# Two FFN down projections of 512 x 2816 x 1024 as seven quadrant products each, one level of Strassen

## The chip, the cores and the metric

The program runs on one core of a Trainium2 chip. The metric is the device time of one execution in microseconds (us). The engines that the text names are TensorE (PE, with its weight loads as PEld), VectorE (DVE), ScalarE (ACT), GpSimd (POOL) and SyncE (SP, which here only issues DMAs).

## The reference

The network is one hybrid block followed by a two-layer block. The change touches only the feed-forward part of the second block:

```python
def conv_ffn(h, w_up, conv_w, conv_b, w_down):
    up = h @ w_up
    a, bval = up[..., :D_FF], up[..., D_FF:]
    a = causal depthwise conv of a, width 3, + conv_b
    return (jax.nn.silu(a) * bval) @ w_down          # D_FF = 2816, D_MODEL = 1024

for l in range(2):                                   # 512 tokens
    ... x = x + mixed @ w_out[l]
    h = rms_norm(x, norm_ffn[l])
    x = x + conv_ffn(h, w_up[l], conv_w[l], conv_b[l], w_down[l])
return rms_norm(x, norm_final)
```

All of it is float32. The product `(silu(a) * bval) @ w_down` has 512 tokens, 2816 = 22 x 128 inner columns and 1024 outputs, and there are two of them, one for each layer.

## The kernel before

**Float32 by three passes.** Every operand of a large matrix product is split into two parts, hi (a rounded copy) and lo (the original minus hi). Both parts are held as `float32r`. `passes` (L1810 to L1814) then issues three matmuls: hi by hi, hi by lo and lo by hi. So one 128 x 128 by 128 x 512 product costs three matmuls of 512 columns.

**Weights.** `weight_plan` cuts all weights into chunks. Each chunk is one DMA, mostly 1 MB, and it holds one or two pieces of 128 x 1024 words. SP loads the chunks in the plan's order into two buffers of `raw` (`chunk_load`, L605 to L609). A load waits until the last piece of the chunk two before it has its lo part. ACT makes the hi part of each piece (`split_hi`, L490 to L497), and DVE makes the lo part from `raw` and hi (`split_lo`, L499 to L505). Both go into one of four slots of `whl`. `room_for` lets ACT write piece w once PE has used piece w - 4. Every loop on ACT and DVE calls the split of piece w + 3 when it stands at piece w, so the splits run up to three pieces ahead of PE.

**Up tiles.** For each f2 of 11, PE makes four tiles: `up_a` of columns 2 f2 and 2 f2 + 1, then `up_b` of the same. Each tile is 24 matmuls. ACT copies `up_a` to `apad`, DVE runs the three conv steps (L1782 to L1784), and ACT applies SiLU into `fsil`. DVE multiplies by `up_b` (L1791), ACT writes the hi part into `ff` (L1062) and DVE the lo part (L1793). `ff` is 88 KB of the 96 KB arena in each partition.

**Down projection.** `row_tiles` (L1841) computes 512 x 1024 outputs in eight PSUM banks, one for each of four token blocks (tb) and two column halves. The token block is the stationary operand, and 512 columns of weights are the moving one. One piece holds two inner tiles of one column half, so PE spends 2 x 4 x 3 = 24 matmuls on each piece. In the second half the last eight inner tiles are done token block by token block, so that each row block ends at a different time. `add_rows` (L1549) adds each bank to the residual `x` on DVE. The norm that follows works row block by row block, and PE transposes the rows (L1836) between the row blocks. In the last layer ACT sums squares (L1068 and L1073), POOL takes the root (L668), and ACT and DVE scale the two halves and store them.

**Queues.** POOL has almost nothing in its queue: the roots of the norms (L668, 28 of them), one early split (L672) and one DMA for each layer (L677). SP's queue holds the weight loads in order, and every load stands behind the wait of the one before it.

Of the kernel before, what the change touches and what calls it, by code (L numbers as in the profile page):

```python
# [31 lines left out]
P = 128  # L32
D = 1024
# [9 lines left out]
FT = D_FF // P  # L43
HEAD = 64
# [55 lines left out]
def weight_plan():  # L100
# [34 lines left out]
    for l in range(LAYERS):  # L135
# [17 lines left out]
        rows("w_down_2", l, FT)  # L153
# [3 lines left out]
def build(nc, t, out):  # L157
# [16 lines left out]
    NP_ = len(pieces)  # L174

# [80 lines left out]
    assert at[0] <= top, at[0] - top  # L256
    sel_r = nc.alloc_sbuf_tensor_at("sel_r", [P, 2, P], R, offset=cst_at + 4 * COFF["sel"])
# [76 lines left out]
    ff = over("ff", 0, [P, FT, 2, SEQ], R)  # L334
    xn2 = over("xn2", 88 * K, [P, 2, D])
# [25 lines left out]
    with ctx:  # L361
# [9 lines left out]
        raw_in, s_raw0 = [sem("raw_in0"), sem("raw_in1")], sem("raw_in_first")  # L371
# [73 lines left out]

        def raw_view(w):
# [3 lines left out]
            r = raw[:, c % 2, :]  # L450
# [5 lines left out]
            if kind in ("w_out", "w_out_2", "w_down_2", "dvw"):  # L456
                return r[:, j * 1024:(j + 1) * 1024].rearrange("p (a b) -> p a b", a=2)
# [32 lines left out]
        def split_hi(w):  # L490

            if w >= NP_:
                return
            c = pieces[w][0]
            nc.scalar.wait_ge(raw_in[c % 2], 16 * (c // 2 + 1))
            room_for(w)
            nc.scalar.activation(whl_view(w, 0), raw_view(w), ACT.Copy).then_inc(w_hi, 1)  # L497
# [11 lines left out]

        def resident(stage):  # L510

            name, l, nk = stage
            return W[(name, l, 1, nk - 8)]
# [21 lines left out]
        def row_wait(eng, stage, half, tb):  # L535
# [4 lines left out]
            elif tb < 3:  # L540
                eng.wait_ge(row_full, ROWS.index(stage) * 6 + half * 3 + tb + 1)
# [39 lines left out]
        def chunk_src(c):  # L581
# [10 lines left out]
            if kind in ("w_out", "w_out_2", "w_down_2"):  # L592
# [68 lines left out]
        def _(pool):  # L661
# [3 lines left out]

            for i_, (s, tb) in enumerate(ORDER):
# [7 lines left out]
                if s in (2, 4) and tb == 3:  # L674
                    l = s // 2 - 1
                    pool.wait_ge(v_out, 32 * (l + 1))
                    pool.dma_start(vc[:].rearrange("p r g n -> p (r g n)"), v_dram[l].rearrange("(u r) n -> u (r n)", r=TB)).then_inc(v_class, 16)  # L677


        @block.scalar  # L680
        def _(act):
# [184 lines left out]
            def norm(s):  # L866
# [35 lines left out]
                norm_hi(s, 3)  # L902

            for l in range(LAYERS):
# [136 lines left out]
                for f2 in range(FT // 2):  # L1041
# [15 lines left out]
                    for j in range(2):  # L1057
                        f = 2 * f2 + j
                        key = ("up_b", l, f)
                        split_hi(W[key] + 3)  # L1060
                        await_read(act, key)
                        A(ff[:, f, 0, :], fsil[:, j, :], ACT.Copy).then_inc(ff_hi, 1)  # L1062
                lead(lead_keys(("w_down_2", l, FT)))
            for tb in range(TB):
                act.wait_ge(row_read, row_reads(ROWS[-1], 0, tb))
                if tb >= 2:
                    act.wait_ge(s_sq0, tb - 1)
                A(xn2[:, 0, tb % 2 * 512:tb % 2 * 512 + 512], x[:, tb, 0:512], ACT.Square, accum_out=ssq0[:, tb:tb + 1]).then_inc(s_sq0, 1)  # L1068
            ov = out[0].rearrange("(b p) d -> p b d", p=P)
            act.wait_ge(s_sq0, TB)  # L1070
            for tb in range(TB):
                act.wait_ge(x_ready, 4 * (STAGES - 3) + tb + 1)
                A(xn2[:, 0, tb % 2 * 512:tb % 2 * 512 + 512], x[:, tb, 512:], ACT.Square, accum_out=ssq[:, tb:tb + 1]).then_inc(s_ssq, 1)  # L1073
# [1299 lines left out]
```

## Time and profile before

| | us |
|---|---|
| median of 3 runs (2155.8 to 2156.01) | 2156.01 |
| the profiled execution | 2156.16 |
| its span | 2154.3 |

| engine | busy us | share of the span |
|---|---|---|
| PE | 2129.8 | 99% |
| DVE | 1276.6 | 59% |
| ACT | 781.4 | 36% |
| POOL | 26.6 | 1% |

The busy time of PE is that of overlapping matmuls. How many microseconds of PE a matmul is worth is read from the distance between two starts, not from its duration. The granted TensorE clock is at its full level (9 in tenths, which is 90% or more) in all 40 slices of the page. DMA moves 101 GB/s on average. In the waits, "A <- B" means that A was idle until B released it.

### The profile page before, as it was taken

The page shows a single profiled execution, that of the slowest core. Times are in us where ns is not written, and L with a number is a line of the kernel's source. Part 1 is how long each engine was busy: PE and PEld are TensorE (multiplying, and loading weights), DVE is VectorE, ACT ScalarE, POOL GpSimd, SP SyncE. Part 2 cuts the span into 40 slices and gives each one's busy share as a digit, 9 for nine tenths or more (in the row PEclk, how much of TensorE's full clock was granted, in tenths as well). Part 3 has the DMA queues.
Part 4 walks back from the last instruction along what each step waited for, and adds up shares of the span by engine and source line. Part 5 has one row for each costly group of instructions (what it writes and reads, how often), then busy time and mean ns, then how long its engine had stood idle before and what let it go on. Part 6 is the DMA issues. An engine that isn't in the chain of part 4 may idle for free.

```text
span 2154.3 us, 24865 instructions
## 1 busy us (share of the span) xinstructions
PE 2129.8 (99%) x10315; PEld 1757.6 (82%) x10315; DVE 1276.6 (59%) x1649; ACT 781.4 (36%) x1036; POOL 26.6 (1%) x41
## 2 busy tenths in 40 slices
PE   7999999999999999999999999999999999999998
PEld 4888888888888887888888888888788888888887
DVE  6899897953665848535665554234853566555422
ACT  3323232223343344444343333135444434333312
POOL 1000000000000100000000000000000000000000
PEclk9999999999999999999999999999999999999999
DMA  9432232233332322322223233223231222323222
GB/s 315 146 118 84 98 103 83 98 117 98 98 93 95 111 79 79 130 67 94 83 84 113 79 109 103 91 69 98 79 137 61 97 78 91 105 83 113 99 88 78
DMA packets 181588, 217.73 MB, mean 101 GB/s; under 512 B 3932, under 2 KB 153316, under 8 KB 181220
## 3 DMA queue, kind: packets, MB, share of 16 engines
q1 hardware_dynamic: 178080, 209.47, 29.5%
q10 hardware_dynamic: 2948, 4.52, 0.6%
q8 instruction: 82, 1.34, 0.3%
q0 software_dynamic: 448, 2.15, 0.3%
q14 instruction: 30, 0.25, 0.0%
HBM read 211.93 MB, written 4.19 MB: 100 GB/s over the span
## 4 chain that ended last, share of the span: by engine, by line
PE 94%; DVE 4%; issue 1%; DMA 1%; ACT 1%; POOL 0%; SPq 0%; POOLq 0%; ACTq 0%; DVEq 0%
PE psum L1812 30%; PE psum L1813 30%; PE psum L1814 30%; DVE whl L504 1%; PE psum L2225 1%; DMA ada<-in_w_ada 1%; PE psum L2257 1%; PE psum L2237 1%; PE psum L2180 0%; PE psum L2210 0%; PE psum L2196 0%; PE psum L1836 0%; PE psum L1955 0%; DVE mrow L1686 0%; POOL stat L668 0%
## 5 line engine op out<-in xcount | busy, mean ns | idle before, releaser
L1812 PE MATMUL psum<-hT,whl 128*128 128x512 f32 (+1 forms) x2064 | 789.1, 382 | 2.8 <-DVE whl L504 1.5
L1814 PE MATMUL psum<-hT,whl 128*128 128x512 f32 (+1 forms) x2064 | 783.1, 379 | 0.0
L1813 PE MATMUL psum<-hT,whl 128*128 128x512 f32 (+1 forms) x2064 | 783.0, 379 | 0.0
L504 DVE TENSOR_TENSOR whl<-raw,whl 128x1024 fp32r<-128x1024 f32 x361 | 438.5, 1217 | 419.5 <-ACT whl L497 419.3
L497 ACT ACTIVATE whl<-raw 128x1024 fp32r<-128x1024 f32 x361 | 376.8, 1047 | 421.3 <-PE psum L1814 386.8
L1812 PEld LDWEIGHTS psum<-hT,whl 128*128 128x128 f32 x2064 | 388.1, 188 | 83.4 <-issue 6.7
L1814 PEld LDWEIGHTS psum<-hT,whl 128*128 128x128 f32 x2064 | 388.2, 188 | 73.7
L1813 PEld LDWEIGHTS psum<-hT,whl 128*128 128x128 f32 x2064 | 388.3, 188 | 71.2 <-issue 0.2
L1812 PE MATMUL psum<-whl,ff 128*128 128x512 f32 x352 | 137.1, 389 | 0.0
L1814 PE MATMUL psum<-whl,ff 128*128 128x512 f32 x352 | 136.9, 389 | 0.0
L1813 PE MATMUL psum<-whl,ff 128*128 128x512 f32 x352 | 136.9, 389 | 0.0
L1812 PE MATMUL psum<-whl,hT 128*128 128x512 f32 (+1 forms) x320 | 112.2, 351 | 0.2 <-DVE whl L504 0.2
L1813 PE MATMUL psum<-whl,hT 128*128 128x512 f32 (+1 forms) x320 | 111.0, 347 | 0.0
L1814 PE MATMUL psum<-whl,hT 128*128 128x512 f32 (+1 forms) x320 | 111.0, 347 | 0.0
L1251 DVE SCALAR_TENSOR_TENSOR hc<-glu,vcol,hc 128x512 f32<-128x512 f32 x120 | 89.9, 750 | 0.0
L1782 DVE TENSOR_SCALAR facc<-apad,vcol 128x512 f32<-128x512 f32 x44 | 24.0, 546 | 110.9 <-ACT fsil L1056 53.0
L1251 DVE SCALAR_TENSOR_TENSOR acc<-glu,vcol,acc 128x512 f32<-128x512 f32 x112 | 84.0, 750 | 0.1
L1050 ACT ACTIVATE apad<-psum 128x512 f32<-128x512 f32 x44 | 26.4, 599 | 146.0 <-PE psum L1814 146.0
L1814 PEld LDWEIGHTS psum<-whl,ff 128*128 128x128 f32 x352 | 66.1, 188 | 13.8
L1813 PEld LDWEIGHTS psum<-whl,ff 128*128 128x128 f32 x352 | 66.1, 188 | 13.7
L1812 PEld LDWEIGHTS psum<-whl,ff 128*128 128x128 f32 x352 | 66.1, 188 | 13.5
L1812 PEld LDWEIGHTS psum<-whl,hT 128*128 128x128 f32 x320 | 60.6, 189 | 8.5 <-issue 0.8
(309 smaller groups left out, 2106.9 us busy)
## 6 DMA issues: line engine op xcount, KB each, us to landing
raw<-in_w_in SPq DMA_DIRECT2D x87, 1024.0 KB, 5.1
raw<-in_w_up SPq DMA_DIRECT2D x44, 1024.0 KB, 5.1
raw<-in_w_down SPq DMA_DIRECT2D x20, 1024.0 KB, 5.0
raw<-in_w_branch SPq DMA_DIRECT2D x12, 1024.0 KB, 5.1
raw<-in_w_out SPq DMA_DIRECT2D x12, 1024.0 KB, 5.0
ada<-in_w_ada SPq DMA_DIRECT2D x8, 1024.0 KB, 9.7
ada<-in_w_ada SPq DMA_DIRECT2D x8, 512.0 KB, 11.1
x<-in_x SPq DMA_DIRECT2D x4, 512.0 KB, 5.6
```

The costliest lines, as they stand in the source:

```text
L497: nc.scalar.activation(whl_view(w, 0), raw_view(w), ACT.Copy).then_inc(w_hi, 1)
L504: nc.vector.tensor_tensor(whl_view(w, 1), raw_view(w), whl_view(w, 0).bitcast(F), ALU.subtract).then_inc(w_lo, 1)
L1050: A(apad[:, j, 2:], bank(W_BANK[key]), ACT.Copy).then_inc(act_read, 1)
L1251: last[dst is acc1] = step(V.scalar_tensor_tensor(A_(dst), g[:, k:k + SEQ], col("cf_w", 8 * k + tt), A_(dst), ALU.mult, ALU.add))
L1782: link(V.tensor_scalar(facc[:], apad[:, j, 2:2 + SEQ], cw(2), col("conv_b", FT * l + f), ALU.mult, ALU.add))
L1812: M(out_, stat_hi, mov_hi, start=start, stop=False, **kw)
L1813: M(out_, stat_hi, mov_lo, start=False, stop=False, **kw)
L1814: return M(out_, stat_lo, mov_hi, start=False, stop=stop, **kw)
L2225: ins = M(bank(2 + e)[:, a:z], qd[heads, g, j, b * P:(b + 1) * P], kd[heads, g, j, k0:k0 + z - a], start=True, stop=True, skip_group_check ...
L2237: ins = nc.tensor.transpose(bank(tb + e)[:, c * P:(c + 1) * P], prob[:, e, c * P:(c + 1) * P], ident)
L2257: ins = M(o_, v, probT[:, e, c * P:(c + 1) * P], start=c in (first_, 2), stop=c in (1, 3), skip_group_check=True)
```

## The change

**Seven products.** The inner tiles are taken in 11 pairs kk, an even tile (t = 0) and an odd one (t = 1). Tokens are cut in halves of 256, output columns in halves of 512. B(t, h) is the 128 x 512 quadrant of the weights in tile t and half h. For each pair there are four kinds of pieces:

- `sA`: B(0, 0) and B(1, 0), as loaded. Two products, with tokens 0 to 255.
- `sB`: T1 = B(0, 1) - B(0, 0), and T4 = B(1, 1) - B(1, 0) - T1. Two products, with tokens 256 to 511, where the even tile's half has been replaced by the sum of the even and odd tiles.
- `sC`: T2 = B(0, 0) + T3, and B(1, 1). Two products, with token sums.
- `sD`: T3 = B(1, 1) - B(0, 1). One product, with a token sum. A piece of `sD` holds two pairs, one of them only one.

A product is two token blocks by three passes, so 6 matmuls of 512 columns. PE's order in `quad_tiles` is all `sA` and `sB` in turn, then all `sC`, then all `sD`.

**Who makes the weight sums.** POOL makes T1 and T4 with two instructions of 1024 and 512 columns, the second behind the first. DVE makes T3 with one of 512 columns, behind the lo part of `sA`. POOL makes T2 in place with one of 512 columns, after all T1 and T4. The splits of all pieces stay on ACT and DVE.

**Loads.** A `quad` chunk (1 MB) holds all four quadrants of a pair and serves `sA`, `sB` and T3. It goes to one of three raw buffers, the third of which lies in the space of `hT` and is free only after the last up tile. Its buffer is released when T1, T4 and T3 are made. `diag` chunks (1 MB for two pairs, by two DMAs) load B(0, 0) and B(1, 1) again for `sC`.

**Token sums.** In the up tiles DVE makes, for each f2, four more instructions (256, 256, 512 and 768 columns) and ACT one of 768. POOL stores the 768 KB that result to DRAM. ACT loads them back into the place of `ff` tiles that PE is done with, one for each pair, during `sA` and `sB`.

**Residual.** `x` (2 MB) goes to DRAM at the start of the up tiles, its space serves for sums, and POOL loads it back after its third T1 and T4. Partial sums of PSUM are added to `x` between the products.

```diff
+        for kk in range(PAIRS):
+            add("w_down_2", ("quad", l, kk), [("sA", l, kk), ("sB", l, kk)], 1024)
+        for i in range(0, PAIRS, 2):
+            add("w_down_2", ("diag", l, i), [("sC", l, k) for k in range(i, min(i + 2, PAIRS))], 1024)
...
     def split_hi(w):
+            if key[0] == "sB":
+                nc.scalar.wait_ge(t_sum, PAIRS * key[1] + key[2] + 1)
+            elif key[0] == "sC":
+                nc.scalar.wait_ge(t2_done, PAIRS * key[1] + key[2] + 1)
+            elif key[0] == "sD":
+                nc.scalar.wait_ge(t3_done, PAIRS * (key[1] + 1))
...
+            def raw_released(c):                                   # SP, before a load
+                if held[0] == "quad":
+                    sp.wait_ge(t_sum, PAIRS * held[1] + held[2] + 1)
+                    sp.wait_ge(t3_done, PAIRS * held[1] + held[2] + 1)
+                elif held[0] == "diag":
+                    sp.wait_ge(w_lo, W[("sC", held[1], min(held[2] + 1, PAIRS - 1))] + 1)
...
+                def t1_and_t4(kk):                                 # GpSimd
+                    pool.wait_ge(raw_in[RAW_BUF[c]], RAW_NEED[c])
+                    if kk == 0: ...                                # x stored and its norm done
+                    elif kk == 1:
+                        pool.wait_ge(w_used, W[("up_b", l, FT - 1)] + 1)
+                    elif kk > 2:
+                        pool.wait_ge(w_lo, W[("sB", l, kk - 2)] + 1)
+                    nc.gpsimd.tensor_tensor(tsum_of(kk), q[:, :, 1, :], q[:, :, 0, :], ALU.subtract).then_inc(pool_chain, 1)
+                    pool.wait_ge(pool_chain, PAIRS * l + kk + 2)
+                    nc.gpsimd.tensor_tensor(tsum_of(kk)[:, 1, :], tsum_of(kk)[:, 1, :], tsum_of(kk)[:, 0, :], ALU.subtract).then_inc(t_sum, 1)
+                def t2(kk):
+                    pool.wait_ge(t3_done, PAIRS * l + kk + 1)
+                    nc.gpsimd.tensor_tensor(b11, b11, t3_of(kk), ALU.add).then_inc(t2_done, 1)
+                for kk in range(PAIRS - 1):
+                    store(kk)
+                t1_and_t4(0)
+                t1_and_t4(1)
+                store(PAIRS - 1)
+                t1_and_t4(2)
+                pool.wait_ge(s_stored, 16 * PAIRS * (l + 1))
+                pool.wait_ge(w_lo, W[("sB", l, 0)] + 1)
+                pool.dma_start(x[:]..., x_dram[l]).then_inc(x_moved, 16)
+                for kk in range(3, PAIRS):
+                    t1_and_t4(kk)
+                for kk in range(PAIRS):
+                    t2(kk)
...
+                for w in range(W[("sA", l, 0)], W[("sC", l, PAIRS - 1)] + 1):     # VectorE, quad_rows
+                    split_lo(w + 3)
+                    if ahead == ("sB", l, 1):
+                        t3(0)
+                        t3(1)
+                    elif ahead[0] == "sA":
+                        t3(ahead[2])
+                    ...                                            # adds of PSUM banks to x
...
+                    V.tensor_tensor(fsil[:, 0, 256:], fsil[:, 0, 256:], fsil[:, 1, 256:], ALU.add).then_inc(s_sums, 1)
+                    link(V.tensor_tensor(ssum[:, 0:256], fsil[:, 0, 256:], fsil[:, 0, 0:256], ALU.subtract))
+                    V.tensor_tensor(ssum[:, 256:768]..., ALU.subtract).then_inc(s_sums, 1)
+                    V.tensor_tensor(sstage[:, 1, :], ssum[:], sstage[:, 0, :].bitcast(F), ALU.subtract).then_inc(s_lo, 1)
...
+                def sums_back(kk):                                 # ScalarE
+                    act.wait_ge(w_used, W[("sB", l, kk)] + 1)
+                    act.wait_ge(s_stored, 16 * (PAIRS * l + kk + 1))
+                    if kk >= 2:
+                        act.wait_ge(s_back[kk % 2], back_count(l, kk - 2))
+                    act.dma_start(ff_r[:, kk, 0:1536].bitcast(F), s_dram[l, kk]).then_inc(s_back[kk % 2], 16)
...
+                def whole_row(tb):                                 # VectorE, rows 2 and 3, after sD
+                    add(tb, 0, 6 + i).then_inc(quad_read, 1)
+                    add(tb, 1, 6 + i).then_inc(x_ready, 1)
...
-                row_tiles(("w_down_2", l, FT), lambda k: ff[:, k, 0, :], lambda k: ff[:, k, 1, :], (ff_lo, FT * l))
+                quad_tiles(l)
```

## Rows read from the trace of the kernel before

**Rows 1.** The page: PE in the down projections, the first of three passes.

```profile
L1812 PE MATMUL psum<-whl,ff 128*128 128x512 f32 x352 | 137.1, 389 | 0.0
```

**Rows 2.** Windows: both up stages and both down stages, busy time of each engine.

```profile
core 0: us, PE busy (x) PEld busy (x) DVE busy (x) ACT busy (x) POOL busy (x), PEclk, DMA share, GB/s
1093.00:1328.80 235.80, 235.53 (x1111) 197.94 (x1110) 129.16 (x156) 82.74 (x111) 0.00 (x0) 1.00 0.30 99
1328.80:1449.00 120.20, 120.20 (x540) 99.71 (x539) 33.10 (x34) 29.27 (x31) 1.65 (x3) 1.00 0.26 88
2027.00:2147.60 120.60, 120.60 (x533) 99.85 (x532) 34.63 (x40) 27.48 (x37) 1.65 (x3) 1.00 0.26 90
```

**Rows 3.** Timeline of PE in layer 0's down projection: start, us, engine, line.

```profile
1446.20 0.39 PE L1814 MATMUL psum<-whl,ff 128*128 128x512 f32 x1
...
1449.83 0.39 PE L1812 MATMUL psum<-whl,ff 128*128 128x512 f32 x1
```

**Rows 4.** Groups by line and shape, DVE and POOL: count, busy us, mean ns, idle before.

```profile
L504 DVE TENSOR_TENSOR whl<-raw,whl 128x1024 fp32r<-128x1024 f32 x357 | 435.8, 1223 | 419.5 <-ACT whl L497 419.3
L1793 DVE TENSOR_TENSOR ff<-fsil,ff 128x512 fp32r<-128x512 f32 x44 | 30.5, 693 | 30.8 <-ACT ff L1062 30.8
L1558 DVE SCALAR_TENSOR_TENSOR x<-psum,x 128x512 f32<-128x512 f32 x32 | 21.3, 686 | 24.0 <-PE psum L1814 24.0
L672 POOL TENSOR_TENSOR whl<-raw,whl 128x512 fp32r<-128x512 f32 x1 | 1.3, 1275 | 13.3 <-DVE stat L1164 13.3
```

**Rows 5.** Timeline of POOL: four of its 28 roots, and its one wide instruction.

```profile
25.81 1.27 POOL L672 TENSOR_TENSOR whl<-raw,whl 128x512 fp32r<-128x512 f32 x1 [13.28 <-DVE stat L1164]
719.07 1.52 POOL L668 TENSOR_TENSOR stat<-stat 128x1 f32<-128x1 f32 x1 [691.98 <-DVE stat L1109]
737.01 1.46 POOL L668 TENSOR_TENSOR stat<-stat 128x1 f32<-128x1 f32 x1 [5.55 <-DVE stat L1472]
751.38 0.55 POOL L668 TENSOR_TENSOR stat<-stat 128x1 f32<-128x1 f32 x1 [8.13 <-DVE stat L1472]
1440.19 0.55 POOL L668 TENSOR_TENSOR stat<-stat 128x1 f32<-128x1 f32 x1 [4.90 <-DVE stat L1472]
```

**Rows 6.** Timeline of DVE at the same five moments.

```profile
26.78 0.85 DVE L1188 TENSOR_TENSOR hT<-utmp,hT 128x512 fp32r<-128x512 f32 x1
...
718.90 1.28 DVE L1508 SCALAR_TENSOR_TENSOR x<-x,stat,lnrow 128x1024 f32<-128x1024 f32 x1
...
736.85 1.22 DVE L1488 TENSOR_TENSOR hT<-xn,hT 128x1024 fp32r<-128x1024 f32 x1
...
751.22 0.68 DVE L1500 TENSOR_TENSOR prod<-psum,table 128x512 f32<-128x512 f32 x1
...
1440.02 1.22 DVE L1484 TENSOR_TENSOR xn<-psum,vcol 128x1024 f32<-128x1024 f32 x1
```

**Rows 7.** DMA: two early windows, then issues with KB and us to landing.

```profile
10.00:20.00 10.00, 5.72 (x14) 1.41 (x15) 6.34 (x14) 4.81 (x7) 1.10 (x2) 1.00 1.06 375
20.00:30.00 10.00, 9.02 (x49) 5.32 (x47) 7.87 (x12) 5.50 (x8) 1.27 (x1) 1.00 1.08 364
...
raw<-in_w_down SPq DMA_DIRECT2D x20, 1024.0 KB, 5.0
```

**Rows 8.** Timeline of ACT in layer 0's down projection: a split's hi part.

```profile
1340.18 1.06 ACT L497 ACTIVATE whl<-raw 128x1024 fp32r<-128x1024 f32 x1 [4.38 <-PE psum L1814]
```

**Rows 9.** The tail of the last row block, and the boundary of the layers.

```profile
2148.04 0.69 DVE L1558 SCALAR_TENSOR_TENSOR x<-psum,x 128x512 f32<-128x512 f32 x1 [2.38 <-PE psum L1814]
2148.76 0.63 ACT L1073 ACTIVATE xn<-x 128x512 f32<-128x512 f32 x1 [3.13 <-DVE x L1558]
2149.52 0.16 DVE L1583 SCALAR_TENSOR_TENSOR stat<-stat 128x1 f32<-128x1 f32 x1 [0.79 <-ACT xn L1073]
...
1454.24 1.15 ACT L860 ACTIVATE xn<-x,stat 128x1024 f32<-128x1024 f32 x1 [0.85 <-POOL stat L668]
...
1457.81 1.04 PE L1836 MATMUL psum<-cst,xn 128*128 128x128 f32 x8
```

More of the change, by code:

```diff
@@ L174, in build @@
     NP_ = len(pieces)
+    key_of = list(W)
+    RAW_BUF, RAW_NEED, RAW_PREV = [], [], []
+    loads, holder = [0, 0, 0], [None, None, None]
+    other = 0
+    for c, (_, key, _) in enumerate(chunks):
+        if key[0] == "quad":
+            b = other if key[2] % 3 == 0 else 1 - other if key[2] % 3 == 1 else 2
+        elif key[0] == "diag":
+            b = (2, other, 1 - other)[key[2] // 2 % 3]
+        else:
+            b = other
+        RAW_BUF.append(b)
+        RAW_PREV.append(holder[b])
+        holder[b] = c
+        loads[b] += 2 if key[0] == "diag" else 1
+        RAW_NEED.append(16 * loads[b])
+        if key[0] not in ("quad", "diag"):
+            other = 1 - b
     W_BANK = {}
@@ L508, in build @@
         ROWS = [("w_out", None, KT)] + [s for l in range(LAYERS) for s in (("w_out_2", l, KT), ("w_down_2", l, FT))]
+        PLAIN = [stage for stage in ROWS if stage[0] != "w_down_2"]
         def resident(stage):
             name, l, nk = stage
-            return W[(name, l, 1, nk - 8)]
+            return W[("sD", l, 2)] if name == "w_down_2" else W[(name, l, 1, nk - 8)]
         def lead_keys(stage):
@@ L1057, in _ @@
                     for j in range(2):
[L1058 to L1063, printed above, removed]
+                        split_hi(W[("up_b", l, 2 * f2 + j)] + 3)
+                    act.wait_ge(s_sums, 2 * (PAIRS * l + f2) + 1)
+                    for j in range(2):
+                        A(ff[:, 2 * f2 + j, 0, :], fsil[:, j, :], ACT.Copy).then_inc(ff_hi, 1)
@@ new lines, in _ @@
+                for w in range(W[("sA", l, 0)], W[("sD", l, 0)] + 1):
+                    split_hi(w + 3)
+                    if key_of[w][0] == "sA" and key_of[w][2]:
+                        sums_back(key_of[w][2] - 1)
+                    if key_of[w] == ("sC", l, 0):
+                        sums_back(PAIRS - 1)
+                    if l == LAYERS - 1 and key_of[w] in (("sC", l, 4), ("sC", l, 5)):
+                        first_square(key_of[w][2] - 4)
+            ov = out[0].rearrange("(b p) d -> p b d", p=P)
@@ L1068, in _ @@
[L1068 to L1073, printed above, removed]
+                    first_square(tb)
```

335 lines of the change are left out of this document (301 added, 34 removed).

## The prediction

> **What bounds the kernel now.** I read the engines' shares first: PE is busy for 99% of the span. Then I read the windows by stage [rows 2]. In both down stages PE is busy for the whole window, 120.2 of 120.2 us and 120.6 of 120.6, while DVE has 33 to 35 us of work and ACT 27 to 29. In an up stage DVE has 129 us of 236. So a matmul taken away is time taken away, as long as the pieces of weights still come in time. A matmul shows 0.39 us, but two of them overlap. Between two starts that are 16 matmuls apart lie 3.63 us [rows 3], so one is worth 0.227 us. The granted clock is at its full level everywhere [rows 2], even in early windows where PE has only 5.7 us of work in 10 [rows 7], so I give short gaps of PE no price in clock.
>
> **What is removed.** Before, the two projections have 3 x 352 = 1056 matmuls [rows 1], 48 for each pair of inner tiles. Seven products of 6 are 42. So 22 pairs save 132 x 0.227 = 29.9 us, 15.0 for each layer. A layer's floor is then 462 x 0.227 = 104.8 us: 59.9 for sA and sB (5.44 for each pair), 29.9 for sC, 15.0 for sD.
>
> **What each piece now costs beside PE.** PE used to spend 24 matmuls, 5.44 us, on a piece. Now it spends 12, 2.72 us. ACT's hi part takes 1.06 us [rows 8] and DVE's lo part 1.22 [rows 4], less than 2.72, so the splits alone keep up. But the sums come on top. For each pair of sA and sB (5.44 us):
> - DVE: two lo parts and T3. T3 has no row. The nearest one is a 512-wide DVE instruction with two SBUF inputs, 0.69 us [rows 4]. Back to back these cost about 0.05 less each: 3.0 us in all.
> - POOL: T1 and T4 (1024 columns), then the second step (512). The 512-wide instruction took 1.27 us [rows 4]. For 1024 there is no row. It is at least 1.27 plus DVE's increment for 512 columns more (1.22 - 0.69 = 0.53), 1.8, and at most twice 1.27, 2.55. I take 2.4, near the double, since the single instruction shows little fixed cost. Together 3.7 us.
>
> Each engine alone is under 5.44. The question is whether they run side by side, and here the trace speaks. POOL's root normally takes 0.55 us. At 719.07 and 737.01 it took 1.52 and 1.46 [rows 5]. Just before each, DVE had started an instruction whose two inputs both lie in SBUF (L1508, L1488), and these ended at 720.18 and 738.07 [rows 6]. POOL ended 0.4 us after each of them. Beside DVE instructions with one input in PSUM (L1500, L1484) it took 0.55. So POOL stands still while DVE reads two SBUF tensors. The other direction shows once: a 512-wide DVE instruction that starts at 26.78, before POOL's wide one ends at 27.08, takes 0.85 us instead of 0.69 [rows 4 to 6]. That is a sign, not a proof.
>
> The Trainium skill, page "SBUF — State Buffer", section "Who interferes with whom", states both directions: a VectorE instruction with two SBUF inputs and a GpSimd instruction that reads SBUF exclude each other for the whole instruction. The rows agree with the first direction. By that rule the sum is the one I make below, and without it the sum is that of rival B. The page "GPSIMD Engine Reference", section 3.1, gives 4497 ns for 2048 float32 columns. An estimate from that page and the 1.27 us row by a straight line is 2.35 us for 1024 columns, against my 2.4, and the sum would stay the same.
>
> **The sum with exclusion.** All lo parts, T3, T1, T4 and T2 read two SBUF tensors. Per pair 3.0 + 3.7 = 6.7 us, less about 0.15 of start for each of the two POOL instructions, plus about 0.2 for handing over: 6.6 us against PE's 5.44. The ends are 6.0 (1024 columns at 1.8) and 7.0.
> - Start. When the last up tile ends (0), POOL starts T1 and T4 of pair 1. It could not before, since its space is in hT. DVE then has the last up pair before it: a 256-wide sum, a lo part, 256- and 512-wide sums, two 512-wide lo parts and the 768-wide one, some 5 us with two SBUF inputs, and POOL 3.7. The lo part of sB(1), the fourth piece, is ready at 9.7 where PE wants it at 8.2. T3 of pairs 0 and 1 is behind it, at 10.5 to 11.5. Only then does SP load pairs 3 and 4. They land 5.0 us later [rows 7], 1 or 2 more beside the return of x. Until then 6.4 us of exclusive work for pair 2 and the same for pair 3 have to pass. sB(3) starts at about 24 instead of 19.0: 5 us late.
> - Seven more pairs up to sB(10): 7 x (6.6 - 5.44) = 8.1 late.
> - sC: one lo part and one T2 are 1.2 + 1.3, about 2.7 with handing over, against PE's 2.72. 1.0 late.
> - sD: the DVE add that frees PSUM bank 6 stands behind a split on DVE, so PE waits about 0.6.
>
> Together 14.7 of 15.0 us for each layer: the gain is eaten, 0.3 a layer is left, 0.6 in all.
>
> **What else is added.** *Tail:* row block 3 now ends with two adds (0.69 each [rows 9]) instead of one, two squares of 0.63 on ACT, and a gain of 0.69 on DVE before the root can be asked for. Some of this overlaps. Before, 1.6 us lie from the start of the add to the end of L1583 [rows 9]. Now I count 2.6, so +1.0. *Boundary of the layers:* row 3 was scaled at 1455.39 and transposed at 1457.81 [rows 9], 2.4 us of slack, which covers one more add. Row 2 has less, so I put +0.7 (0 to 2). *Up stage:* four DVE instructions, about 0.4 + 0.4 + 0.7 + 0.95 = 2.5 us for each f2 of 21.4, beside 11.7 us of DVE work (129.16 / 11 [rows 2]). They are hidden, and so are ACT's 0.8 us and POOL's stores. ACT now waits for the sums before the split for the next f2, but that split is asked for some 15 us before PE wants it. If this cover failed, each f2 would show it, 22 times. *Wait for x* (DVE, first f2): 2 MB written while PE has 21 us of tiles, hidden. *Loads back on ACT's queue:* the waits in front of each (PE done with the pair, stored, the load two before it landed) are met as long as DMA keeps up. Behind them stand the hi parts. If one came late, PE would stall by as much.
>
> Sum: 2156.16 - 29.9 + 2 x 14.7 + 1.0 + 0.7 = 2157.4. The profiled execution lies 0.15 above the median, so against the median it is the same to 0.2. I say 2157.5.
>
> **The rivals.**
> - *A, exclusion at 6.2 to 7.0 us a pair (0.55).* The case above. Each 0.1 us on a pair moves the two layers by 1.4 us. Its own range is 2151 to 2164.
> - *B, no exclusion of DVE by POOL (0.26).* For it: DVE's delay shows once and by 0.16 us only. Against: POOL's delay is plain, and a shared path should work both ways. Then the sums keep up, and PE is late only at the start (3), by sD (0.6) and by DMA. DMA then has to bring 1.05 + 0.79 MB for each 5.44 us, 338 GB/s, and 2 MB of x once. Windows of before show 364 to 375 [rows 7], so about 2 us late. 2156.2 - 29.9 + 2 x 5.6 + 1.7 = 2139. If DMA were the wall, up to 2146. The range is 2134 to 2146.
> - *C, handing over is dear (0.19).* POOL ended its root 0.4 us after DVE let go [rows 5, 6]. With two or three such handings for each pair the cycle is 7.5 us, and the loads of later pairs, which wait for T1, T4 and T3, move with it. Late: 5 + 7 x 2.06 + 2.5 + 0.6 = 22.5, 7.5 more than the saving. 2156.2 + 2 x 7.5 + 1.7 = 2173, slower. It decides from a cycle of about 6.9 us on. The range is 2165 to 2182.
>
> **How the numbers follow.** The likeliest case is A, so 2157.5. About 4.3 us (0.2%) is what a measurement of this kernel can tell from no change, so "same" is 2151.7 to 2160.3. Of A's 0.55 I put 0.05 below, 0.29 within and 0.21 above that band. B is wholly faster, C wholly slower: faster 0.31, same 0.29, slower 0.40. The range of 8 in 10 has to take in most of B and of C: 2137 to 2175. The likeliest case's own range is 2151 to 2164.
>
> **What would show each step.** PE: 924 matmuls in the down projections. In sA and sB, the distance from sB(k) to sB(k + 1): 5.44 in B, about 6.6 in A, 7.5 in C. PE's waits there should name DVE's lo part, and behind it POOL's T1 and T4. A POOL instruction that overlaps a lo part should be longer than one that does not, and a DVE lo part that starts under a POOL one should show more than 1.22 us. If the lo parts stay at 1.22 beside POOL, A is wrong. The 1024-wide POOL instruction should take 2.4 us when alone. If PE's waits name DMA, it is the wall in B. The up stages should keep their 235 us. A longer one would break the step that I cost at nothing. The tail after the last matmul should be 7.7 instead of 6.7 us.

## The result, and the profile after

| | before | after |
|---|---|---|
| median, us | 2155.99 | 2178.09 (2174.57 to 2179.04, 4 runs) |
| span of the profiled execution | 2154.3 | 2176.5 |
| ratio of the times | 1 | 1.0101 (95% interval 1.0086 to 1.0114) |

The change makes the kernel 22 us slower, 3 us above the upper end of the range. First the page of the kernel after: the engines, DMA, the chain that ended last by engine, and of the costliest groups DVE's lo parts and PE's first passes in the down projections (busy, mean ns, idle before and its releaser).

```profile
PE 2117.6 (97%) x10183; PEld 1737.3 (80%) x10183; DVE 1457.7 (67%) x1812; ACT 832.3 (38%) x1092; POOL 182.2 (8%) x133
...
DMA packets 188854, 272.27 MB, mean 125 GB/s; under 512 B 5052, under 2 KB 154436, under 8 KB 187972
...
PE 85%; DVE 9%; DMA 2%; issue 1%; ACT 1%; POOL 1%; SPq 0%; POOLq 0%; ACTq 0%; DVEq 0%
...
L577 DVE TENSOR_TENSOR whl<-raw,whl 128x1024 fp32r<-128x1024 f32 x361 | 455.2, 1264 | 286.1 <-ACT whl L570 285.8
...
L2110 PE MATMUL psum<-whl,ff 128*128 128x512 f32 x176 | 73.5, 418 | 25.8 <-DVE whl L577 25.7
```

The last line answers to [rows 1]: 176 instead of 352, with a mean of 418 ns instead of 389. With the 132 of `sC` and `sD` (output `psum<-whl,ff_r`) these are 308 first passes, 924 matmuls. The 29.9 us of matmuls are gone, as worked out. In their place PE sat idle, 25.8 us in front of these first passes alone, and it was DVE's lo part (L577) that ended 25.7 of them. [rows 1] shows 0.0 there.

**The steady state.** Timeline of PE in layer 0 (only the lines with a wait), then DVE and POOL beside it:

```profile
1380.67 0.50 PE L2110 MATMUL psum<-whl,ff 128*128 128x512 f32 x1 [0.44 <-DVE whl L577]
1386.85 0.50 PE L2110 MATMUL psum<-whl,ff 128*128 128x512 f32 x1 [0.40 <-DVE whl L577]
```

```profile
1380.55 1.21 DVE L577 TENSOR_TENSOR whl<-raw,whl 128x1024 fp32r<-128x1024 f32 x1
1381.68 2.88 DVE L1779 TENSOR_TENSOR ff_f<-raw 128x512 f32<-128x512 f32 x1
1384.48 2.31 DVE L577 TENSOR_TENSOR whl<-tsum,whl 128x1024 fp32r<-128x1024 f32 x1
1386.72 1.21 DVE L577 TENSOR_TENSOR whl<-raw,whl 128x1024 fp32r<-128x1024 f32 x1
```

```profile
1380.76 3.25 POOL L789 TENSOR_TENSOR tsum<-raw 128x1024 f32<-128x1024 f32 x1 [1.23 <-DVE whl L577]
1384.09 1.62 POOL L791 TENSOR_TENSOR tsum<-tsum 128x512 f32<-128x512 f32 x1
1386.94 3.25 POOL L789 TENSOR_TENSOR tsum<-raw 128x1024 f32<-128x1024 f32 x1 [1.23 <-DVE whl L577]
```

Read the two engines by time. At 1380.76 POOL starts under DVE's lo part, which ends at 1381.76. POOL then needs another 2.25 us, to 1384.01. T3 (L1779) starts on DVE at 1381.68 and ends 0.55 us after POOL has ended, 2.88 us for an instruction that takes 0.68 alone. The next lo part starts under POOL's second step and takes 2.31 instead of 1.22. DVE has no idle time, and PE gets a pair every 6.17 us (1380.67 to 1386.85) instead of every 5.44.

**The start.** POOL in layer 0's down projection, from the return of `x` on, then windows (us, PE busy, PEld, DVE, ACT, POOL, granted clock, DMA share, GB/s), then PE's waits in the first 50 us (one of 0.35 left out):

```profile
1342.37 0.58 POOL L809 DMA_DIRECT2D x<-x_kept  x1
1346.35 2.36 POOL L789 TENSOR_TENSOR tsum<-raw 128x1024 f32<-128x1024 f32 x1 [3.40 <-DMA raw<-in_w_down]
1348.80 2.16 POOL L791 TENSOR_TENSOR tsum<-tsum 128x512 f32<-128x512 f32 x1
1358.74 2.35 POOL L789 TENSOR_TENSOR tsum<-raw 128x1024 f32<-128x1024 f32 x1 [7.78 <-DMA raw<-in_w_down]
```

```profile
1093.00:1328.80 235.80, 235.54 (x1111) 197.93 (x1110) 149.97 (x194) 90.50 (x120) 9.22 (x12) 1.00 0.41 137
1345.00:1350.00 5.00, 5.00 (x16) 3.96 (x15) 3.46 (x3) 1.06 (x1) 3.57 (x2) 0.66 1.02 424
1350.00:1355.00 5.00, 5.00 (x23) 4.12 (x23) 2.73 (x2) 1.06 (x1) 0.96 (x1) 1.00 0.99 412
1355.00:1360.00 5.00, 2.04 (x10) 1.35 (x8) 0.22 (x1) 1.06 (x1) 1.26 (x1) 1.00 1.03 421
1360.00:1365.00 5.00, 2.68 (x7) 2.14 (x8) 4.43 (x3) 1.67 (x2) 4.92 (x3) 0.73 0.57 183
```

```profile
1338.56 0.50 PE L2110 MATMUL psum<-whl,ff 128*128 128x512 f32 x1 [1.17 <-DVE whl L577]
1344.26 0.47 PE L2110 MATMUL psum<-whl,ff 128*128 128x512 f32 x1 [2.68 <-DVE whl L577]
...
1362.32 0.74 PE L2110 MATMUL psum<-whl,ff 128*128 128x512 f32 x1 [5.27 <-DVE whl L577]
...
1374.50 0.50 PE L2110 MATMUL psum<-whl,ff 128*128 128x512 f32 x1 [1.53 <-DVE whl L577]
```

`x` (2 MB) is asked back at 1342.37. From 1345 to 1360 the DMA engines are full (share 0.99 to 1.03, 412 to 424 GB/s). The load of pair 3, issued at 1341.39 ahead of `x`, lands in 4.9 us. That of pair 4, issued at 1343.05, lands at 1358.67, 15.6 us later. POOL waits 7.78 us for it, and behind POOL PE waits 5.27. "PE <- DVE" is only the last link. After each of the longer waits the clock is lower: 0.66 in the window after 2.68 us, with 16 matmuls in 5 us where full speed has 22, and 0.73 after 5.27. The first window answers to [rows 2]: the up stage has 21 us more of DVE work, PE has the same 1111 matmuls in it and no idle time, and the down projection starts at 1329.0 us as before.

**The boundary of the layers and the tail**, PE then DVE:

```profile
1461.61 1.97 PE L2134 MATMUL psum<-cst,xn 128*128 128x128 f32 x8 [2.83 <-ACT xn L1011]
1465.04 0.55 PE L2110 MATMUL psum<-whl,hT 128*128 128x256 f32 x1 [1.46 <-DVE whl L577]
```

```profile
1454.82 1.23 DVE L1672 TENSOR_TENSOR hT<-xn,hT 128x1024 fp32r<-128x1024 f32 x1 [1.13 <-ACT hT L1015]
1455.97 1.22 DVE L1668 TENSOR_TENSOR xn<-psum,vcol 128x1024 f32<-128x1024 f32 x1
1457.10 1.28 DVE L1783 SCALAR_TENSOR_TENSOR x<-psum,x 128x512 f32<-128x512 f32 x2
...
2169.31 1.29 DVE L1783 SCALAR_TENSOR_TENSOR x<-psum,x 128x512 f32<-128x512 f32 x2 [1.46 <-PE psum L2112]
```

The adds of row 2 (L1783) could have run from 1451.4 on. They stand behind three instructions for rows 0 and 1 and start at 1457.10, and PE waits 2.83 us for row 2 and 1.46 behind that. Before, no wait above 0.2 us stands there. Over the ten us from 1460 the granted clock is 0.66. In the tail the last matmul starts at 2168.89 and the span ends at 2176.5: 7.6 us instead of 6.7 [rows 9].

**The balance.** Distances between starts of matmuls beyond 0.227 us: idle gaps 18.1 us in layer 0's down projection and 17.2 in layer 1's, matmuls at a slower clock 4.4 and 4.3, boundary 6.8, tail 0.9. These are 51.7. Less the 29.9 saved, 21.8 of the 22.2 us between the spans are found. The gaps count by distance, so each is a little longer than the idle time in brackets.

### The profile page after: what moved, and what is told of

The parts are those of the page before. It is cut to its first block, busy times and chain, and to the rows that moved or that the text cites. A ratio compares the mean times of both kernels' runs of the same rounds, so it can differ in the third digit from the quotient of the medians.

```text
span 2176.5 us, 25150 instructions
## 1 busy us (share of the span) xinstructions
PE 2117.6 (97%) x10183; PEld 1737.3 (80%) x10183; DVE 1457.7 (67%) x1812; ACT 832.3 (38%) x1092; POOL 182.2 (8%) x133
## 4 chain that ended last, share of the span: by engine, by line
PE 85%; DVE 9%; DMA 2%; issue 1%; ACT 1%; POOL 1%; SPq 0%; POOLq 0%; ACTq 0%; DVEq 0%
PE psum L2110 27%; PE psum L2112 27%; PE psum L2111 27%; DVE whl L577 4%; DVE ff_f L1779 1%; DMA raw<-in_w_down 1%; PE psum L2609 1%; DMA ada<-in_w_ada 1%; PE psum L2641 1%; PE psum L2621 1%; PE psum L2564 0%; PE psum L2594 0%; PE psum L2580 0%; DVE t_first L1779 0%; ACT whl L570 0%
## 5 line engine op out<-in xcount | busy, mean ns | idle before, releaser
L577 DVE TENSOR_TENSOR whl<-raw,whl 128x1024 fp32r<-128x1024 f32 x361 | 455.2, 1264 | 286.1 <-ACT whl L570 285.8
L817 POOL TENSOR_TENSOR stat<-stat 128x1 f32<-128x1 f32 x28 | 21.1, 754 | 1180.4 <-DVE stat L1293 708.7
L2110 PE MATMUL psum<-whl,ff 128*128 128x512 f32 x176 | 73.5, 418 | 25.8 <-DVE whl L577 25.7
L2111 PE MATMUL psum<-whl,ff 128*128 128x512 f32 x176 | 71.5, 406 | 0.0
L2112 PE MATMUL psum<-whl,ff 128*128 128x512 f32 x176 | 71.1, 404 | 0.0
L1222 ACT ACTIVATE ff<-fsil 128x512 fp32r<-128x512 f32 x44 | 25.4, 624 | 119.3 <-DVE fsil L2076 119.3
L2074 DVE TENSOR_TENSOR fsil<-psum,fsil 128x512 f32<-128x512 f32 x44 | 30.2, 687 | 60.2 <-PE psum L2112 60.2
```

The source lines that it names most:

```text
L577: nc.vector.tensor_tensor(whl_view(w, 1), raw_view(w), whl_view(w, 0).bitcast(F), ALU.subtract).then_inc(w_lo, 1)
L1222: A(ff[:, 2 * f2 + j, 0, :], fsil[:, j, :], ACT.Copy).then_inc(ff_hi, 1)
L2074: V.tensor_tensor(fsil[:, j, :], bank(W_BANK[key]), fsil[:, j, :], ALU.mult).then_inc(dve_read, 1)
L2110: M(out_, stat_hi, mov_hi, start=start, stop=False, **kw)
L2111: M(out_, stat_hi, mov_lo, start=False, stop=False, **kw)
L2112: return M(out_, stat_lo, mov_hi, start=False, stop=stop, **kw)
```

## The experiments

The experiments ran on three chips, each beside runs of the kernel before on its own chip. The medians of those are 2155.96 to 2156.04 us, so times from different chips can be compared.

### POOL that only writes

```diff
-                    nc.gpsimd.tensor_tensor(tsum_of(kk), q[:, :, 1, :], q[:, :, 0, :], ALU.subtract).then_inc(pool_chain, 1)
...
-                    nc.gpsimd.tensor_tensor(tsum_of(kk)[:, 1, :], tsum_of(kk)[:, 1, :], tsum_of(kk)[:, 0, :], ALU.subtract).then_inc(t_sum, 1)
+                    for i_m in range(3):
+                        nc.gpsimd.memset(tsum_of(kk), 0.25).then_inc(pool_chain, 1)
...
+                    nc.gpsimd.memset(tsum_of(kk)[:, 1, :], 0.25).then_inc(t_sum, 1)
...
-                    nc.gpsimd.tensor_tensor(b11, b11, t3_of(kk), ALU.add).then_inc(t2_done, 1)
+                    nc.gpsimd.memset(b11, 0.25).then_inc(t2_done, 1)
```

> T1, T4 and T2 are not computed: GpSimd fills their places by memsets (three of 1024 columns and one of 512 for T1 and T4, one of 512 for T2) behind the same waits, so the weight sums are left out and GpSimd reads no SBUF tensor. Theory 1 (DVE instructions with two SBUF inputs and GpSimd instructions that read SBUF exclude each other, in both directions): the lo parts and T3 go back to 1.22 and 0.69 us even under a GpSimd instruction, the distance between two pairs falls from 6.17 to 5.44 us, which is 5 to 6 us a layer, and the start gets 2 to 3 us a layer better: some 2160 us in all. Theory 2 (what costs is the chain through T1, T4, hi and lo, not the shared path): the lo parts stay short only if GpSimd is short; the cycle follows GpSimd's own time for T1 and T4, so with GpSimd busy for less than 3.7 us a pair nothing can be told, and with 3.7 or more it stays near 6.17: 2175 to 2178 us.

Measured: 2145.55 us (ratio to before 0.995, 0.9935 to 0.9965), 32.5 less than after. The weight sums are left out, so this is not a kernel to use. DVE's groups from 1329 to 1420 us (us busy, mean ns):

```profile
L577 DVE TENSOR_TENSOR whl<-raw,whl 128x1024 fp32r<-128x1024 f32 x21 | 25.7, 1224 | 19.5 <-ACT whl L570 19.5
L577 DVE TENSOR_TENSOR whl<-tsum,whl 128x1024 fp32r<-128x1024 f32 x10 | 12.2, 1225 | 12.7 <-ACT whl L570 12.7
L1780 DVE TENSOR_TENSOR ff_f<-raw 128x512 f32<-128x512 f32 x8 | 5.5, 684 | 0.0
```

POOL is nearly as busy per pair (three times 0.96 and once 0.53 us, 3.4 against 3.7 for the two sums when nothing blocks them), but it reads nothing. Every lo part takes 1.22 us and T3 0.68 (mean 2.47 in the kernel after). The steady waits are gone, and of the start's five waits one of 2.29 us is left. So it is POOL's reading of SBUF, not its being busy, that costs DVE. The gain is twice what I expected, because the start improved too: POOL and T3 are done earlier, the load of pair 4 is asked for 5.9 us earlier (1337.17), and although `x` comes back beside it and it takes 13.7 us, it is in time but for that one wait.

### The return of x, later

```diff
-                pool.dma_start(x[:]..., x_dram[l]).then_inc(x_moved, 16)
                 for kk in range(3, PAIRS):
                     t1_and_t4(kk)
+                    if kk == 8:                                # was: ahead of pair 3
...
+                        pool.dma_start(x[:]..., x_dram[l]).then_inc(x_moved, 16)
```

> One edit: GpSimd loads x back after T1 and T4 of pair 8 instead of pair 2. Theory 1 (the 2 MB of x take the DMA engines from the loads of pairs 3 to 5, while DMA moves 412 to 424 GB/s): the waits of PE before pairs 4 and 5 (5.3 and 5.1 us, one a layer) fall below 1 us and the stretch at a lower granted clock behind them goes: 12 us less in all, 2166 us. Theory 2 (the load of pair 4 is late because its buffer is released late, behind T3 of pair 1 on DVE): the waits shrink by less than 2 us a layer: 2174 to 2178 us.

Measured: 2166.19 us (1.0049, 1.0034 to 1.0064), as expected. PE's waits at the start (and the new one):

```profile
1344.31 0.47 PE L2111 MATMUL psum<-whl,ff 128*128 128x512 f32 x1 [2.68 <-DVE whl L577]
1355.27 0.50 PE L2111 MATMUL psum<-whl,ff 128*128 128x512 f32 x1 [0.88 <-DVE whl L577]
```

The wait of 5.27 us has become 0.88, and the load of pair 4 takes 8.6 us instead of 15.6. The same bytes at the wrong moment were worth 12 us in two layers. A part comes back at `sC`. `x` itself is there long before DVE adds to it: it is asked for at 1379.88 and takes 11.7 us, and the first add starts at 1400.91. But the loads for `sC` that run beside it are late. POOL waits for them with T2,

```profile
1401.77 1.29 POOL L799 TENSOR_TENSOR raw<-raw,t_first 128x512 f32<-128x512 f32 x1 [3.14 <-DMA raw<-in_w_down]
```

ACT's hi parts wait for POOL, DVE's lo parts for ACT, the adds stand behind the lo parts, and PE waits 2.71 us for an add at 1406.07.

### Row 2 ahead of the gains of rows 0 and 1

```diff
+                whole_row(2)
                 gained(s, 0)
                 norm_lo(s, 0)
+                statistics(2)
                 gained(s, 1)
-                whole_row(2)
-                statistics(2)
```

> One edit at the boundary of the layers: on DVE the two adds of row block 2 stand before the norm work of row blocks 0 and 1 instead of behind it, and its statistics behind the first lo part. Theory 1 (row block 2 waits in DVE's queue, from 1451.4 to 1457.1 us in the profile of the changed kernel): PE's wait of 2.8 us for the scaled rows shrinks to about 0.7, and the low granted clock behind it gets shorter: 3 to 5 us less, 2173 to 2175 us. Theory 2 (the two row buffers of the norm bind: the square of row block 2 needs the lo part of row block 0): less than 1.5 us less.

Measured: 2175.6 us (1.0092, 1.0076 to 1.0109), 2.5 less, with single runs of the two kernels that overlap. PE's wait of 2.83 us is 0.91, and the one behind it has grown from 1.46 to 2.35. Of the 6.8 us of the boundary the place of the adds explains no more than 2.5.

### All weight sums on DVE

T1, T4 and T2 move from POOL's queue to DVE's, each ahead of the split that needs it. The arithmetic is unchanged.

```diff
+                    if ahead[0] == "sA":
+                        t1_and_t4(ahead[2], l)                 # V.tensor_tensor instead of nc.gpsimd
...
+                    elif ahead[0] == "sC" and ahead[2] + 2 < PAIRS:
+                        t2(ahead[2] + 2, l)
                     split_lo(w + 3)
```

> GpSimd makes no sums: DVE makes T1 and T4 of pair k ahead of the lo part of sA(k), and T2 two pairs ahead of its lo part. Nothing is left out. Theory 1 (exclusion): no instruction is stretched, DVE needs 2 x 1.17 + 0.65 + 1.17 + 0.65 = 4.8 us a pair, under PE's 5.44, so the distance between pairs falls from 6.17 to about 5.45 us although DVE has more to do, 5 to 6 us a layer; the start is the same or up to 2 us worse: 2164 to 2170 us. Theory 2 (DVE's in-order queue and its total work are what costs): a distance of 6.2 us or more, 2178 us or slower.

Measured: 2159.49 us (1.0017, 1.0008 to 1.0026), 18.6 less than after. Steady state, the columns as above:

```profile
1375.00:1405.00 30.00, 30.00 (x134) 24.86 (x133) 27.01 (x33) 11.68 (x11) 0.00 (x0) 1.00 0.96 337
```

DVE alone does what both did before: 27.0 us of work in 30, no wait of PE. On DVE the wide sum takes 1.22 us, and on POOL it took 2.35 and stopped DVE for as long. Left are waits of 1.56, 1.23 and 5.48 us at the start, the last again behind a late load.

### The same, with x back behind pair 5

```diff
+                pool.wait_ge(t_sum, PAIRS * l + 5 + 1)
...
                 pool.dma_start(x[:]..., x_dram[l]).then_inc(x_moved, 16)
```

> e4 (all weight sums on DVE) with one more edit: x is loaded back when the sums of pair 5 are made instead of at the start. Theory 1 (the return of x starves the weight loads): the wait of 5.5 us at pair 3 in each layer goes to under 1 us, and with it the stretch at a lower granted clock (about 1.5 us): 12 to 14 us less than e4, 2146 us. Theory 2 (the loads of pairs 3 and 4 are late by their own release behind T3 on DVE): less than 4 us less, 2156 us or more.

Measured: 2155.48 us (0.9996, 0.9987 to 1.0005): 4.0 us of the expected 13. The wait of 5.48 is gone, but the adds to `x` come late (waits of 1.87 and 0.95 us in layer 0, 3.08 in layer 1). `x` itself has landed at 1369.39, 24 us before the first add. What the adds stand behind in DVE's queue is a T2 that waits 1.68 us for its weights (1390.46). Here my picture was too simple: I had taken the return of `x` for a burst that only has to be placed well.

### DVE alone, start and boundary reordered

On DVE the sums of pair 1 and the split of `sB(1)` go ahead of the last up pair's lo parts, on ACT the hi part of `sB(1)` ahead of that of the last token sums. The adds of rows 0 and 1 and the boundary are reordered.

> e5 with the start, the end of sC and the boundary of the layers put in another order. Start: T1 and T4 of pair 1 and the lo part of sB(1) go ahead of the last token sums' lo parts on DVE and the hi part likewise on ACT. Boundary: PE transposes row block 0 in the middle of sD and row block 2 behind the first value tile; DVE adds row block 2 ahead of the gain of row block 1. End of sC: two adds ahead of a lo part. Nothing is left out. If the change is sound and only its feeding was late: no PE wait over 0.5 us in either down stage, granted clock back to 1.00, and the sum is 2156 - 29.9 + 1 (tail) + 1 to 3 = 2128 to 2131 us. If something else eats the gain (matmuls slower with new operands, DMA), it stays above 2138 us.

Measured: 2149.83 us (0.9971, 0.9961 to 0.9982): faster than the kernel before by 6 us, and the fastest here that computes everything, but 20 above what I expected. Windows, the columns as above:

```profile
1345.00:1390.00 45.00, 42.87 (x187) 34.61 (x186) 37.87 (x42) 17.72 (x17) 0.54 (x1) 1.00 1.02 404
1390.00:1420.00 30.00, 26.41 (x116) 21.23 (x115) 23.91 (x29) 10.61 (x10) 0.00 (x0) 1.00 0.57 197
```

```profile
1394.15 0.47 PE L2123 MATMUL psum<-whl,ff_r 128*128 128x512 f32 x1 [2.11 <-DVE x L1787]
1397.27 0.50 PE L2123 MATMUL psum<-whl,ff_r 128*128 128x512 f32 x1 [1.48 <-DVE x L1787]
```

For 45 us the DMA share is 1.02. DVE's queue waits for loads of weights (1.91 us at 1389.84), and the adds stand behind that. The experiment without the return of x, below, tests whether this is the cause.

### The kernel before, with gaps put in

```diff
+                    for i_g in range((12, 25)[l]):
+                        ins = nc.gpsimd.memset(neghalf, -0.5).then_inc(gap_chain, 1)
...
+                    nc.gpsimd.memset(neghalf, -0.5).then_inc(gap_done, 1)
...
+                pe.wait_ge(gap_done, l + 1)                    # ahead of the down projection
```

> The kernel before, with two waits put into PE at the start of the down projections, where GpSimd runs a chain of small memsets: 12 in layer 0, 25 in layer 1. It measures what an idle stretch of PE costs beyond itself. Theory 1 (the granted clock falls after an idle stretch and takes a while to come back): the matmuls behind the longer gap start 0.45 us apart instead of 0.227 for some us, and the time grows by more than the two gaps, by 1 to 3 us. Theory 2 (the slower stretches in the changed kernel come from elsewhere): the time grows by exactly the gaps and the clock stays at 1.00.

Measured: 2167.0 us (1.005, 1.0036 to 1.0064), 11.0 more for waits of 2.12 and 4.18 us:

```profile
1331.00:1336.00 5.00, 4.78 (x14) 3.80 (x15) 1.44 (x2) 0.44 (x1) 0.10 (x2) 0.66 0.39 122
1336.00:1341.00 5.00, 5.00 (x24) 4.13 (x23) 1.23 (x1) 1.06 (x1) 0.00 (x0) 1.00 0.23 87
2031.00:2036.00 5.00, 1.16 (x6) 0.62 (x4) 2.63 (x4) 1.58 (x2) 2.43 (x24) 0.85 0.20 79
2036.00:2041.00 5.00, 4.66 (x11) 3.69 (x12) 0.00 (x0) 0.00 (x0) 0.20 (x2) 0.50 0.63 211
2041.00:2046.00 5.00, 5.00 (x22) 4.08 (x22) 0.39 (x1) 1.06 (x1) 0.00 (x0) 0.97 0.00 0
```

Nothing else changed, so the two waits cost 4.7 us beyond their own length. By the matmuls' distances 4.1 of these are the clock: behind the waits the matmuls start 0.43 us apart instead of 0.227. After 4.18 us of idleness PE worked at 0.50 of the full clock, that is at the lower level, 1.2 GHz, for about 5 us, with 11 matmuls for 22. After the 2.12 us the granted clock was 0.66 over 5 us.

### GpSimd kept, with the best of the rest

The kernel after, `x` back behind pair 5, the boundary as in `e6_dve_all`.

> The changed kernel, sums on GpSimd as before, with x loaded back after pair 5 and the boundary of the layers in the order of e6. By exclusion the distance between pairs stays 6.17 us, and the starts keep their 1.2 and 2.7 us of waits: against e2's 2166 us it gains what the boundary gave (6 to 7 us with the clock) and the wait for x of 2.7 us a layer: 2152 to 2157 us, level with the kernel before. If exclusion were a small matter it would come near e6, below 2140 us.

Measured: 2168.38 us (1.006, 1.0045 to 1.0076), 9.7 less than after, not the 21 or more that I expected. The cycle of 6.17 us stays, and so do three of the start's waits (1.17, 2.68, 1.52) and those in front of the adds (1.03 and 0.61, as 1.05 and 0.63 in the kernel after). I had also counted on winning back 2.7 us a layer of waiting for `x`, and in `e2_x_back_late` PE had not waited for `x` itself. With `x` behind pair 5 a load is late there: POOL waits 3.87 us for it at 1377.47, and PE 1.53. At the boundary the wait has only moved, from ACT's scaled row (2.83) to a weight piece (3.20). With POOL's sums kept, everything that I reordered left the kernel slower than before, and all of it together no faster than `e2_x_back_late` alone.

### The DVE kernel without the return of x

```diff
-                pool.dma_start(x[:]..., x_dram[l]).then_inc(x_moved, 16)
+                for tb in range(TB):
+                    nc.gpsimd.memset(x[:, tb, :], 0.25).then_inc(pool_chain, 1)
...
-                        dve.wait_ge(x_moved, 32 * l + 32)
+                        dve.wait_ge(pool_chain, 4 * l + 5)
```

> The kernel of e6_dve_all, but x does not come back from DRAM: GpSimd fills it with a constant by four memsets of 1024 columns instead, so the residual is left out of the two down projections and the output is another. Per layer 2 MB less for DMA; nothing else changes. Theory 1, the transfers are the wall of e6_dve_all: its rows moved 396 to 407 GB/s at a share of 1.02, so 2 MB are worth about 5.2 us of transfers per layer, and PE's waits behind late loads in layer 0 (0.61, 0.42, 2.11 and 1.48 us) and in layer 1 (1.08, 2.04 and 3.32) should fall below 1 us each; 11 us of waits less, no gain beyond that from the clock: 2140 (2136 to 2143), against 2149.8. Theory 2, those waits come from the order of DVE's own queue (sums, splits and adds of banks back to back): they stay, and the time is 2148 to 2151.

Measured: 2137.1 us (0.9912, 0.9897 to 0.9927), 12.7 less for 2 MB less in each layer. PE's first passes in layer 0's down projection (the last few of `sD` are outside the window), here and then in `e6_dve_all`:

```profile
L2124 PE MATMUL psum<-whl,ff 128*128 128x512 f32 x88 | 34.4, 391 | 1.1 <-DVE whl L577 1.1
...
L2124 PE MATMUL psum<-whl,ff_r 128*128 128x512 f32 x64 | 25.2, 394 | 0.0
```

```profile
L2123 PE MATMUL psum<-whl,ff_r 128*128 128x512 f32 x62 | 24.6, 397 | 3.6 <-DVE x L1787 3.6
```

DVE's queue has the same work in the same order. Its wait of 1.91 us for a load is 0.28 here, and of PE's waits behind it none is left. In `e6_dve_all` `x` had landed at 1368.24, 25 us before the first add, so it was not waited for either. So transfers are the wall of the DVE version, and not the order of its queue. 12.7 us for 4.2 MB are 3.0 us for each MB, somewhat more than the 2.5 that one takes at 404 GB/s.

### The DVE kernel with x in four parts and an earlier split

```diff
+                for part, kk in enumerate((2, 4, 6, 8)):
+                    pool.wait_ge(t_sum, PAIRS * l + kk + 1)
+                    pool.dma_start(x[:, part, :], x_dram[l][:, part * D:(part + 1) * D]).then_inc(x_moved, 16)
...                                                            # ACT: the same with split_hi(w0 + 4)
                 statistics(2)
+                split_lo(w0 + 4)
                 norm_lo(s, 1)
-                split_lo(w0 + 4)
```

> The kernel of e6_dve_all with two more changes and the full computation. (a) x comes back in four DMAs of 512 KB, behind the sums of pairs 2, 4, 6 and 8, instead of one of 2 MB behind pair 5. (b) At the boundary of the layers ACT makes the hi part, and DVE the lo part, of the first weight piece of the next stage ahead of norm_hi(1) and norm_lo(1). For (b) PE's wait of 3.31 us there should fall below 1 us: 3 to 4 us less. For (a): if the sum of the bytes is the wall, spreading them moves waits without removing them, 0 to 2 us less; if the burst is what starves the loads, 5 us less and more. Theory 1 (sum of bytes): 2145 (2143 to 2147). Theory 2 (burst): 2140 (2138 to 2142).

Measured: 2150.78 us (0.9978, 0.9969 to 0.9987), the same as `e6_dve_all`. Spreading the 2 MB changed nothing, PE still waits 3.20 and 1.12 us for the adds to `x`. That speaks once more for the sum of the bytes and against the burst, though two changes ran in one kernel. The 4 us that I expected of the other change did not come. At the boundary the wait of 3.31 us for the first piece is 0.19, and the second piece now has 2.57 us. ACT and DVE have more to do there between the last `sD` pieces and the next stage than PE leaves them time for. Which of them it is, I haven't settled.

## Why the prediction was wrong, point by point

The mechanism of the likeliest case, exclusion, is there and nearly in its forecast size. What failed are three terms beside it: the load of pair 4, priced at 6 or 7 us and measured at 15.6, waits of PE without a price in clock, measured at 8.7 us in two layers, and the boundary at 0.7, measured at 6.8.

- **The matmuls removed: right.** 924 of them, 29.9 us.
- **Exclusion of DVE and POOL in both directions: right, and shown.** The lo part takes 1.21 us alone and 2.31 under POOL, and 1.22 again when POOL only writes. With the sums on DVE the cycle is PE's 5.44 again. The Trainium skill, page "SBUF — State Buffer", section "Who interferes with whom", also says that a GpSimd instruction that only writes does not contend; the 1224 ns beside memsets agree. The single row of 0.85 for 0.69 from which I doubted the second direction was too weak a sign: rival B deserved less than 0.26.
- **The prices on POOL: right.** 2.35 us alone for 1024 columns against my 2.4. Handing over, rival C's ground, costs nothing to be seen: T3 ended 0.55 us after POOL. So C came nearest to the time, and its range holds it, by a mechanism that isn't there. Its cycle was 7.5.
- **The cycle, 6.6 against 6.17 measured: close, too high by the 0.2 for handing over and more.** Seven pairs were to cost 8.1 us. Only five ran in this steady state, at 0.73 each, 3.6.
- **The load of pair 4, "5.0 us, 1 or 2 more beside the return of x": the step that failed most inside a layer.** Up to sB(3) the start went nearly as I had it: it began 25.2 us after the first matmul (1354.16) against my "about 24". Of its 6.1 us late 3.9 are two waits from exclusion (1.17 and 2.68), and some 1.6 the clock behind them. But I then let seven pairs run at the steady cycle. The load of pair 4 took 15.6 us instead of 6 or 7, and PE waited 5.27, then 0.35 and 1.53, so that the two pairs behind sB(3) came 9.5 us late instead of 2.3. Two things made that load late, and either one removed takes most of the wait away: without `x` beside it (e2) 0.88 us are left, and with `x` but with POOL and T3 unblocked (e1) 2.29. I had summed DMA's bytes for rival B only, and in A I let the sums be late while the transfers kept up.
- **"Short gaps of PE no price in clock": wrong.** The cost was 4.4 and 4.3 us in the two layers, and the kernel before with gaps put in shows it alone. I had read 1.00 in the clock's column of [rows 7]. The trace's first record of the clock is at 16.06 us, and up to there the column says nothing. The matmuls of the same windows of the kernel before say more:

```profile
13.39 4.05 PE L1955 MATMUL psum<-ada,stat 128*1 128x512 f32 x6 [9.99 <-DMA ada<-in_w_ada]
...
19.19 3.59 PE L1955 MATMUL psum<-ada,stat 128*1 128x512 f32 x8 [0.89 <-DMA ada<-in_w_ada]
```

Behind a wait of 9.99 us six of them take 4.05 us, and behind one of 0.89 eight of the same kind take 3.59. The first ones start 0.80 to 0.85 us apart, the later ones 0.43. That the lower clock is the reason is my reading, since no run changed this wait, but it was a warning in the trace that I had.
- **The boundary, 0.7 (0 to 2): mis-sized, 6.8 measured.** I priced one more add against the slack of row 3. What came was a whole row of two adds behind three instructions for other rows, and after it a weight piece, a wait behind the wait, and clock again (0.66 from 1460 to 1470). Moving the adds (e3) won 2.5 us of it at most, and for the rest I have only what each wait names, no run that removes it.
- **sC and sD, 1.0 + 0.6: too low, and the cause right.** PE waits 2.4 us there. The last link of PE's waits at sC (1.05 and 0.63) is an add to `x`, but the adds stand behind lo parts that exclusion has stretched (two in 3.45 us at 1405.22). With POOL only writing (e1) or out of it (e4) these two waits are gone. The two at sD (0.44 behind the add that frees a bank, as forecast, and 0.32) stay in both.
- **The tail, +1.0: right, 0.9. The up stages at no cost: right.** 1111 matmuls in 235.8 us as before.

The sum of the misses: a layer lost 22.5 and 21.5 us (idle gaps and clock) against my 14.7, 14.6 more for both. In layer 0, by the distances between the pairs, 1.1 us of the excess arise up to sB(3), 7.2 in the two pairs behind it and 1.8 in sC and sD, and the five steady pairs are 2.2 under my figure. 4.4 us of it are the clock. The boundary adds 6.1, and the tail takes 0.1 off. That is 20.6, the distance from the 31.1 us that I forecast as lost to the 51.7 of the balance.

## What to carry to other kernels

Before moving work to an idle engine, ask what it reads: if its instructions read SBUF and those of DVE have two SBUF inputs, they add up, and the work is cheaper on the faster of the two (here 1.22 us on DVE against 2.35 on POOL, 18.6 us for the kernel). When matmuls are cut, add up the bytes for each remaining microsecond over the whole stage, with every copy that the rearrangement brings along: here one copy of 2 MB in each layer cost 12.7 us in the DVE version, against the 29.9 that the matmuls saved. And price a wait of PE at more than its length where it isn't short: 6.3 us of waits cost 11.0.

## What the runs showed of the hardware that I had not expected

- A wait of PE of 4.18 us was followed by a stretch at the lower level of the clock, 0.50 for 5 us. Two waits of 6.3 us together cost 11.0. The wait of 1.08 us at 1347.07 in `e9_no_x_return` left the granted clock at 1.00 in the window around it (1345 to 1360).
- DMA moved 404 GB/s over 45 us and up to 424 over 5. I had taken the 364 to 375 of [rows 7] for its peak. Even so it was the wall. The Trainium skill, page "DMA: Bandwidth & Descriptors", section "Where 436 GB/s comes from", says that for transfers between HBM and SBUF the HBM side binds at about 358 GB/s, and gives 425 GB/s for one transfer of 16 MB beside it. These windows, with one core running, are above the first and near the second, and the measurement decides.
- Beside the 2 MB of `x` on another queue, four loads of weights from 1340 to 1355 took 13.9 us to land in the median. With `x` later (e2) the same four took 7.9, and loads with nothing beside them 5.0. The urgent queue got no precedence that the rows show.
- Handing over from POOL to DVE costs nothing that the trace shows: T3, blocked until POOL's end at 1384.01, ended 0.55 us later, and it takes 0.68 alone.
